# The first three units of a projection take their input ahead of the norm's factor, which is applied to their banks afterwards

## What is computed

```
for l in range(DEPTH):
    mod = cond @ ada_w[l] + ada_b[l]
    shift, scale, gate = jnp.split(mod, 3, axis=-1)
    h = rms_norm_2(x, norm_g[l]) * (1.0 + scale[:, None, :]) + shift[:, None, :]
    ...
    x = x + gate[:, None, :] * y
# rms_norm_2(x, g) = x * rsqrt(mean(x * x) + EPS) * g
# odd mixer
proj = (h @ w_in).astype(jnp.float32)
q, k, v, g, fl = jnp.split(proj, [FOX_WIDTH, 2 * FOX_WIDTH, 3 * FOX_WIDTH, 4 * FOX_WIDTH], axis=-1)
...
o = o * jax.nn.silu(g)
return o.astype(h.dtype) @ w_out
```

## Time and profile before

| | |
|---|---|
| median of 3 runs | 1335.21 us (1334.97 to 1335.21) |
| profiled execution, its time | 1334.41 us |
| profiled execution, span | 1332.6 us |
| TensorE busy | 1312.1 us, 98% |
| VectorE busy | 924.2 us, 69% |
| ScalarE busy | 809.0 us, 61% |
| GpSimd busy | 127.3 us, 10% |

### The profile page before, as it was taken

How to read it: one execution, slowest core, us unless ns; L and a number is a source line. 1 busy time by engine, 2 the same in 40 slices (tenths; PEclk the granted TensorE clock), 3 DMA queues, 4 the chain that set the end, 5 groups by cost and what they waited for, 6 DMA issues and landing times.

```text
span 1332.6 us, 28059 instructions
## 1 busy us (share of the span) xinstructions
PE 1312.1 (98%) x10516; PEld 1281.2 (96%) x10516; DVE 924.2 (69%) x1506; ACT 809.0 (61%) x1576; POOL 127.3 (10%) x119
## 2 busy tenths in 40 slices
PE   8999999999999999999999999899999999999998
PEld 8999999999999999999999888899999899999898
DVE  7877556976777555877645877688875576576775
ACT  6766555446766565766654665777765453466773
POOL 2000012013000022000021211120002200010000
PEclk9999999999999999999999999999999999999999
DMA  6777554554677473677563543357756353445441
GB/s 242 236 222 224 193 220 156 184 168 155 219 233 219 158 263 110 222 231 217 165 252 111 168 144 100 127 188 239 238 192 254 122 159 95 127 156 185 136 129 62
DMA packets 64580, 240.54 MB, mean 181 GB/s; under 512 B 7840, under 2 KB 9360, under 8 KB 64496
## 3 DMA queue, kind: packets, MB, share of 16 engines
q1 hardware_dynamic: 63408, 238.84, 54.9%
q0 software_dynamic: 1088, 0.53, 0.2%
HBM read 237.70 MB, written 1.05 MB: 179 GB/s over the span
## 4 chain that ended last, share of the span: by engine, by line
PE 89%; DVE 5%; ACT 4%; issue 1%; DMA 1%; SPq 0%; ACTq 0%; DVEq 0%
PE bank L1917 26%; PE bank L1919 26%; PE bank L1918 26%; DVE w_lo L1168 2%; PE bank L1961 1%; PE bank L1968 1%; PE bank L1969 1%; PE bank L2301 1%; DVE h L1230 1%; ACT w_hi L643 1%; DVE arena L1224 1%; PE bank L2285 1%; PE bank L2284 1%; PE bank L2286 1%; ACT ln_t L674 0%
## 5 line engine op out<-in xcount | busy, mean ns | idle before, releaser
L1168 DVE TENSOR_TENSOR w_lo<-raw,w_hi 128x1024 fp32r<-128x1024 f32 (+2 forms) x376 | 493.2, 1317 | 221.6 <-ACT w_hi L643 221.5
L1917 PE MATMUL bank<-x_hl,w_hi 128*128 128x272 f32 (+1 forms) x2008 | 579.3, 288 | 2.1 <-DVE w_lo L1168 1.3
L1919 PE MATMUL bank<-x_hl,w_lo 128*128 128x272 f32 (+1 forms) x2008 | 574.7, 286 | 0.0
L1918 PE MATMUL bank<-x_hl,w_hi 128*128 128x272 f32 (+1 forms) x2008 | 572.3, 285 | 0.0
L643 ACT ACTIVATE w_hi<-raw 128x1024 fp32r<-128x1024 f32 (+2 forms) x376 | 410.2, 1097 | 175.2 <-PE bank L1919 99.9
L1917 PEld LDWEIGHTS bank<-x_hl,w_hi 128*128 128x128 f32 x2008 | 378.0, 188 | 3.2 <-DVE w_lo L1168 1.5
L1918 PEld LDWEIGHTS bank<-x_hl,w_hi 128*128 128x128 f32 x2008 | 380.5, 190 | 0.4
L1919 PEld LDWEIGHTS bank<-x_hl,w_lo 128*128 128x128 f32 x2008 | 377.4, 188 | 0.0
L1917 PE MATMUL bank<-a_hi,w_hi 128*128 128x272 f32 (+1 forms) x960 | 275.8, 287 | 0.9 <-DVE w_lo L1168 0.6
L1919 PE MATMUL bank<-a_hi,w_lo 128*128 128x272 f32 (+1 forms) x960 | 273.5, 285 | 0.0
L1918 PE MATMUL bank<-a_lo,w_hi 128*128 128x272 f32 (+1 forms) x960 | 273.0, 284 | 0.0
(11 more groups left out here) (286 smaller groups left out, 1256.4 us busy)
## 6 DMA issues: line engine op xcount, KB each, us to landing
raw<-w SPq DMA_DIRECT2D x312, 512.0 KB, 4.3
raw<-w SPq DMA_DIRECT2D x64, 704.0 KB, 5.8
ada_raw<-ada_w SPq DMA_DIRECT2D x48, 512.0 KB, 3.6
h<-x_in SPq DMA_DIRECT2D x2, 544.0 KB, 5.3
work<-bands SPq DMA_DIRECT2D x1, 544.0 KB, 6.7
out<-h SPq DMA_DIRECT2D x1, 512.0 KB, 2.9
out<-h SPq DMA_DIRECT2D x4, 128.0 KB, 2.3
arena<-arena POOLq DMA_DIRECT2D x28, 17.0 KB, 3.3
```

Of the source, the lines that this page charges most:

```text
L1168: ve.tensor_tensor(w_lo[:, s, cols], raw[:, s, cols], w_hi[:, s, cols].bitcast(F32), ALU.subtract).then_inc(w_lo_ready, 1)
L1917: te.matmul(dst, w_hi[:, s, a:a + P], rhs_hi, start=first, stop=False)
L1918: te.matmul(dst, w_hi[:, s, a:a + P], rhs_lo, start=False, stop=False)
L1919: return te.matmul(dst, w_lo[:, s, a:a + P], rhs_hi, start=False, stop=last)
```

## The change

The norm's factor is one number for each token, so it can be taken out of the projection: W(h · gs · r + shift) = r · W(h · gs) + W · shift. The change uses this for the first three units of `oin`.

- ScalarE and VectorE round h · gs, without r, to upper and lower halves in the same columns of `x_hi` and `x_lo` (steps b and bl), chunk by chunk, as `h` becomes known.
- The shift is written 8 times side by side into 8 further columns of `x_hi` and `x_lo` (steps sh and sl). The three units' matmuls have 264 columns instead of 256, so that column 256 of each bank holds W · shift.
- VectorE computes gs ahead of `out2`, and sl too. sl waits for sh, and ScalarE does sh behind the four upper halves of `eout`'s second quad.
- TensorE starts the three units when the third lower half of `oin` is there. The two matmuls that sum the squares lie between the second and the third chunk; there are no fillers. GpSimd adds one chunk more.
- For the fourth unit and all later ones the normed input is made as before, over the columns that the three units have read (step hi of a chunk waits for TensorE's step a of this chunk).
- When the three units are done, VectorE multiplies their banks by `r_t` into SBUF (steps m) and copies column 256 into `gate_bias` (steps w), in place of ScalarE's copies c0 to c2. This stands among the lower halves of the units 4 to 6.
- Silu is applied with these biases in three instructions of 256 columns and one of 1280 for the other five gates.

The diff, cut to its core:

```diff
-            if n == "preo":
-                pool.phase(n, [f"add{c}" for c in range(1, 6)])
...
+        def declare_preo():
+            act.phase("preo", ["sh", "sq0", "sq1", "sq2", "b0", "b1", "sq3", "sq4", "b2", "sq5", "b3", "sq6", "b4", "b5", "sq7",
+                               "b6", "b7", "ln", "r"] + names([("hi", c) for c in range(DC)]))
...
             out2("eout", 0)
+            shift = mod[:, 1, 0, :].unsqueeze(2).broadcast_to([P, DC, COL])
+            sc.activation(x_hi[:, :, SEQ:SEQ + COL], shift, ACT.Copy).then_inc(act.step("preo", "sh"), 1)
+
+            def raw_upper(c):
+                sc.activation(x_hi[:, c, 0:SEQ], h[:, c, META:T], ACT.Copy, scale=gs[:, 1, c:c + 1]).then_inc(act.step("preo", f"b{c}"), 1)
+
+            sc.wait_ge(vec.sem, vec.at("preo0", "gs"))
             for c in range(DC):
                 if 4 <= c < 7:
                     split_next("eout", 1, c - 4)
+                if c == 5:
+                    raw_upper(2)
+                if c == 6:
+                    raw_upper(3)
                 pre_square("preo", c, (vec.sem, vec.at("eout", f"h{c % 4}", c // 4)))
-            pre_rms("preo")
+                if c == 2:
+                    raw_upper(0)
+                    raw_upper(1)
+                if c == 6:
+                    raw_upper(4)
+                    raw_upper(5)
+            raw_upper(6)
+            raw_upper(7)
+            rsqrt("preo", STAT[:, 0:SEQ], r_t[:, 0:SEQ], 1.0 / D, eps6, (pe.sem, pe.at("preo", "ss")))
+            split_next("eout", 1, 3)
             for c in range(DC):
+                if c < DC - 1:
+                    sc.wait_ge(pe.sem, pe.at("preo", f"a{c}"))
+                else:
+                    sc.wait_ge(unit_done, SLOTS * FIRST_QUAD["oin"] + BEHIND)
                 pre_upper("preo", c)
-                if c == 4:
-                    split_next("eout", 1, 3)
...
             for u in range(GATES):
-                fox_evict(u)
+                if u >= BEHIND:
+                    fox_evict(u)
                 fox_split_hi(u)
...
-                    sc.activation(gates, gates, ACT.Silu).then_inc(act.step("gates", "sg"), 1)
+                    sc.wait_ge(vec.sem, vec.at("behind", f"w{BEHIND - 1}"))
+                    for v in range(BEHIND):
+                        sc.activation(fox_unit(v), fox_unit(v), ACT.Silu, bias=gate_bias[:, v:v + 1]).then_inc(act.step("gates", f"sg{v}"), 1)
+                    rest_g = gates[:, BEHIND * SEQ:GATES * SEQ]
+                    sc.activation(rest_g, rest_g, ACT.Silu).then_inc(act.step("gates", "sg"), 1)
...
+                    for c in range(DC):
+                        ve.wait_ge(act.sem, act.at("preo", f"b{c}"))
+                        ve.scalar_tensor_tensor(x_lo[:, c, 0:SEQ], h[:, c, META:T], gs[:, 1, c:c + 1], x_hi[:, c, 0:SEQ].bitcast(F32),
+                                                ALU.mult, ALU.subtract).then_inc(vec.step("preo", f"bl{c}"), 1)
                 ve.wait_ge(act.sem, act.at(phase, "r"))
...
-                        if phase == "preo" and c == 4:
+                        if phase == "preo" and c == 0:
                             split_next("eout", 1, 3)
...
+            ve.scalar_tensor_tensor(gs[:, 1, :], mod[:, 1, 1, :], 1.0, par("norm_g", 8, 8), ALU.add, ALU.mult
+                                    ).then_inc(vec.step("preo0", "gs"), 1)
+            ve.wait_ge(act.sem, act.at("preo", "sh"))
+            ve.tensor_tensor(x_lo[:, :, SEQ:SEQ + COL], mod[:, 1, 0, :].unsqueeze(2).broadcast_to([P, DC, COL]),
+                             x_hi[:, :, SEQ:SEQ + COL].bitcast(F32), ALU.subtract).then_inc(vec.step("preo0", "sl"), 1)
             out2("eout", 0)
             pre("preo")
+
+            def fox_behind(u):
+
+                ve.wait_ge(unit_done, SLOTS * FIRST_QUAD["oin"] + u + 1)
+                ve.tensor_tensor(fox_unit(u), fox_bank(u)[:, 0:SEQ], r_t[:, 0:SEQ], ALU.mult).then_inc(vec.step("behind", f"m{u}"), 1)
+                ve.tensor_copy(gate_bias[:, u:u + 1], fox_bank(u)[:, SEQ:SEQ + 1]).then_inc(vec.step("behind", f"w{u}"), 1)
...
             for u in range(GATES):
                 fox_split_lo(u)
+                if u < BEHIND:
+                    fox_behind(u)
...
-            te.wait_ge(pool.sem, pool.at("preo", "add5"))
-            te.matmul(STAT[:, 0:SEQ], ones[:, :], sq8[:, 0, 0:SEQ], start=True, stop=False).then_inc(pe.step("preo", "ss5"), 1)
-            pre("preo", range(6, DC))
-            keep_clock(9, bank[2])
...
                 if u >= 4:
-                    te.wait_ge(act.sem, act.at(f"c{fox_freed(u)}", "c"))
+                    freed = fox_freed(u)
+                    if freed < BEHIND:
+                        te.wait_ge(vec.sem, vec.at("behind", f"w{freed}"))
+                    else:
+                        te.wait_ge(act.sem, act.at(f"c{freed}", "c"))
...
-            first_quad("preo", "oin", SEQ, (bank[0], bank[1], bank[7]))
+            def behind_quad():
+
+                n, q = SEQ + COL, FIRST_QUAD["oin"]
+                te.wait_ge(w_lo_ready, SLOTS * q + BEHIND)
+                te.wait_ge(vec.sem, vec.at("eout", "h3", 0))
+
+                def lower(k):
+                    te.wait_ge(vec.sem, vec.at("preo", f"bl{k}"))
+                    for u in range(BEHIND):
+                        last = te.matmul(fox_bank(u)[:, 0:n], w_hi[:, u, k * P:(k + 1) * P], x_lo[:, k, 0:n], start=False, stop=k == DC - 1)
+                        if k == DC - 1:
+                            last.then_inc(unit_done, 1)
+                    if k < DC - 1:
+                        last.then_inc(pe.step("preo", f"a{k}"), 1)
+
+                for k in range(DC):
+                    te.wait_ge(act.sem, act.at("preo", f"b{k}"))
+                    for u in range(BEHIND):
+                        te.matmul(fox_bank(u)[:, 0:n], w_hi[:, u, k * P:(k + 1) * P], x_hi[:, k, 0:n], start=k == 0, stop=False)
+                        te.matmul(fox_bank(u)[:, 0:n], w_lo[:, u, k * P:(k + 1) * P], x_hi[:, k, 0:n], start=False, stop=False)
+                    if k:
+                        lower(k - 1)
+                    if k == 1:
+                        te.wait_ge(pool.sem, pool.at("preo", "add6"))
+                        te.matmul(STAT[:, 0:SEQ], ones[:, :], sq8[:, 0, 0:SEQ], start=True, stop=False)
+                        te.wait_ge(act.sem, act.at("preo", "sq7"))
+                        te.matmul(STAT[:, 0:SEQ], ones[:, :], sq8[:, DC - 1, 0:SEQ], start=False, stop=True).then_inc(pe.step("preo", "ss"), 1)
+                lower(DC - 1)
+                te.wait_ge(w_lo_ready, SLOTS * q + 4)
+                for k in range(DC):
+                    te.wait_ge(vec.sem, vec.at("preo", f"lo{k}"))
+                    last = product(bank[3][:, 0:SEQ], 3, k, x_hi[:, k, 0:SEQ], x_lo[:, k, 0:SEQ], k == 0, k == DC - 1)
+                last.then_inc(unit_done, 1)
+
+            behind_quad()
```

More of the change, by code:

```diff
@@ L467, in build @@
         vec.phase("fl0", ["wlo0", "wlo1", "ib", "cb", "ob", "o64"])
+        vec.phase("behind", [a + str(u) for u in range(BEHIND) for a in ("m", "w")])
         for u in range(GATES):
-            act.phase(f"c{u}", ["c"])
+            if u >= BEHIND:
+                act.phase(f"c{u}", ["c"])
             if u == 3:
```

25 lines of the change are left out of this document (17 added, 8 removed).

## The result

| | before | changed |
|---|---|---|
| median of 14 runs each, us | 1335.18 (1334.49 to 1336.75) | 1339.3 (1337.63 to 1341.15) |
| profiled execution, us | 1334.41 | 1340.28 |
| its span, us | 1332.6 | 1338.5 |

What follows compares the result with a forecast made beforehand. TensorE, busy for 98% of the span, was taken to bound the kernel. Delays of 3.15 us by unit 6 and 0.6 for Silu gave +3.7, 1338.1 us profiled and 1338.9 median, range 1336.7 to 1341.5.

Steps and rivals of the forecast that it cites:

- Step 1: Ahead of out2: VectorE, held for sh, starts 2.7 us late and TensorE idles before eout's second quad: +1.9 us.
- Step 2: Between eout and oin: first quad waits for three lower halves, not the norm, starting 1182.4 against 1183.02: -0.6 us.
- Step 3: In oin's first quad: 264-column matmuls and two sums of squares make it 9.8 us; +0.1 us in all.
- Step 4: In oin's fourth unit: its input needs r_t, so the unit ends at 1196.0 against 1194.9; +1.1 us in all.
- Step 5: Ahead of unit 6: TensorE waits 1.6 us for ScalarE's late copy of unit 4's bank; +3.15 us in all.
- same: Rival: the late steps prove cheaper, giving 1336.6 to 1337.8 us; chance 0.19.
- Step 6: Ahead of unit 13: Silu in four instructions takes 2.51 us instead of 1.92, with nothing hiding it: +0.6 us.
- The sum: Whole kernel: 3.15 + 0.6 = +3.7 us, profiled execution 1334.41 to 1338.1, median 1338.9 us.
- The clock rival: Rival: up to three TensorE idle stretches without fillers slow the clock, adding 1.5 to 4.5 us: 1340.4 to 1343.4; chance 0.12.
- last sign of being wrong: Closing list: wrong if TensorE has no wait in eout's second quad, none ahead of unit 6, or the granted clock falls.
- Faster: Rival at the border: sh reaches VectorE before TensorE needs the first lower half, first quad 3.4 us early, 1332.3; chance 0.05.

Runs made afterwards that it cites:

- second profile with fillers: Repeat of the changed kernel with seven filler matmuls added between eout's second quad and oin's first quad: 1338.62 us, ratio 1.0026.
- one Silu: Changed kernel with one Silu of 2048 columns without bias instead of three of 256 with bias and one of 1280: 1340.4 us, ratio 1.0031.
- c4 first: Changed kernel with ScalarE's forget gate exp and ln behind unit 6's bank copy and the next upper half: 1336.79 and 1337.85 us.

## Why the prediction was right

**Step 1, the hold: as predicted.** VectorE starts 1171.70 - 1167.87 - 1.13 = 2.70 us late for 2.7, TensorE idles 1.73 for 1.7. Why it costs so much, the two experiments show: alone it is worth 2.7 to 2.8 us, and taken out of the change 2.6.

**Step 2, the hole: right, undersized.** `oin` starts 1.1 us early, not 0.6. The larger term that was off is the further 0.3 us for two more lower halves beside GpSimd's adds: the third lower half starts at 1181.65, which less 1.13 and 2.70 is 1177.82, where it was before. The other 0.2 us is the step from that lower half to TensorE: its record ends at 1183.00, and TensorE starts at 1183.05.

**Step 3, the quad: right at full clock.** 9.7 us for 9.8. In the profiled execution it was 11.3, by the clock.

**Step 4, the fourth unit: 0.3 us too much.** At full clock (second profile with fillers) it ends 0.8 us late for 1.1, since r_t came earlier with step 2. It waits 0.29 and 0.39 us for the last two lower halves, as foretold.

**Step 5, unit 6's bank: right, somewhat too large.** A wait of 1.25 us in the trace, for 1.6; the two units stand 1.5 us further apart than without it. Unit 6 is 37.8 - 35.3 = 2.5 us late at full clock, for 3.15, the 0.5 of step 2 carried on. Taking the wait out gave 1.5 us back. The prediction also has unit 4 wait a little for its bank, which step w0 frees (it names this under "same"). No wait is marked there, but the rows of the changed kernel show it:

```profile
1200.26 0.15 DVE L1759 COPY gate_bias<-bank 128x1 f32<-128x1 f32 x1
1200.55 0.35 PE L1972 MATMUL bank<-x_hl,w_hi 128*128 128x256 f32 x1
```

TensorE's last matmul ahead of it starts at 1200.19. At full clock this adds 0.25 us to the 0.8 of step 4.

**Step 6, Silu: as predicted.** 1.31 and 1.26 us overlap by 0.1 and take 2.47 for 2.51; TensorE's wait is 0.64, and one Silu gives 0.5 back.

**The sum.** At full clock the changed kernel needs 168.7 - 165.4 = 3.3 us more for a forecast of 3.7. From the start of `oin` on, the second profile with fillers splits it like this: 1.1 us gained, then lost 0.6 in the quad, 1.3 in the fourth unit, 0.25 at unit 4's bank, 1.5 at unit 6's, 0.6 at unit 13 and 0.1 behind it. The 6 of the changed kernel's 19 runs with a mean clock of 1.0 have a median of 1338.6, 3.4 above before. The median of all 14 came out 0.4 over the forecast's 1338.9, since the fall of the clock was added in more than half of the executions. It costs 1.6 us in the profile above (37.8 for 39.4 at unit 6). So the mechanism of the sum is borne out, but that the median lies this close is in part luck: steps too dear by 0.4 us stand against a fall of the clock that the sum left out.

**The clock rival was no alternative but an addition.** The prediction's last sign of being wrong, "if the granted clock falls", came true: the forecast held it at full. It gave the rival a chance of 0.12 and a price of 1.5 us for each of up to three stretches. One fall was seen in an execution, behind two stretches, and its price of 1.2 to 1.6 us was near; its chance was set far too low, though the median stayed under the rival's 1340.4, since only a part of the executions has it. The argument for the low chance was the longest idle time in the trace of before, put at 1.21 us with no fall behind it. That is misread by a little, for behind the opening fillers there is a longer one:

```profile
12.87 0.39 PE L1917 MATMUL bank<-x_hl,w_hi 128*128 128x272 f32 x1 [1.27 <-DVE w_lo L1168]
```

It has no fall behind it either. Both rows speak for single stretches shorter than any of the two that the change makes, 1.7 and 1.9 us, and these lie close together.
The Trainium skill, "TensorE: Matmul & The Clock Gate", Part 1, has activity release the throttled clock and an idle TensorE lose it; the trace agrees in that 0.50 was granted for some 3 us behind two idle stretches of under 2 us each, but the fall came when TensorE had been busy again for 1.1 us.

**Same and faster fell.** "Same" needed steps that are cheaper by at least 1.1 us in all; they were cheaper by 0.4. "Faster" needed sh to be over before VectorE is wanted. The kernel without the hold shows what that rival gives with steps 5 and 6 still in it: +0.7 us from the anchor on, no gain. With c4 first as well it is a gain of 0.9 by the profiles, too small for the timed runs to show.

## What to carry to other kernels

An instruction of 0.2 us that waits for another engine costs what stands behind it in its queue: before placing one, look at what its releaser has to do first, and put it as late as its own reader allows. Filling a hole of 5 us in the busiest engine is worth only what the next engine's chain lets through; here the change gained 1.1 us of the 5 and lost 4.4 behind it at full clock, of which 2.6 are marked waits at three later places. Where idle stretches of nearly 2 us lie close together on TensorE, look at the granted clock in short windows, and compare profiles from a row that both share, not by their spans.

## What the hardware showed that was not expected

The granted clock fell to 0.50 behind two idle stretches of 1.7 and 1.9 us, in four of five profiles, 1.0 to 1.5 us after the second had ended, and came back within 3 to 4 us with TensorE busy; matmuls of 264 columns stood 0.22 us apart instead of 0.12, and the price was 1.2 to 1.6 us. One stretch of 1.7, or of 1.3, did not do it at this place in eight profiles, but in one of them a stretch of 1.66 us near the start had a fall behind it. Whether the 1.9 us alone would do it was not run. The same program's position at 1167 us varied by 2.6 us between executions, which is near the size of the whole effect that was to be measured.
